# Moving the tiles that TensorE reads to other byte offsets in SBUF

## What is computed

```
h    = rmsnorm(x, a_norm);            xb, gate = h @ a_w_in           # 2048 -> 2 x 2560
xb   = causal width-4 depthwise conv(xb)
r, i = sigmoid(block_diag(xb, w_r)), sigmoid(block_diag(xb, w_i))     # 10 blocks of 256
y    = linear recurrence over time of (a(r), u(i, xb));  x += (y * silu(gate)) @ a_w_out
k, v = rmsnorm(x, kv_norm) @ w_kv;    q, gate = rmsnorm(x, b_norm) @ b_w_in
o    = stick-breaking attention(q, k, v)                              # 16 heads of 128
x   += (o * silu(gate)) @ b_w_out;    out = rmsnorm(x, final_norm)
```

## The kernel before

| tiles | offset modulo 512 |
|---|---|
| `stage`, `w_hi`, `w_lo`, `x_hi`, `x_lo`, `ident` | 128 |
| `y_hi`, `y_lo`, `o_hi`, `o_lo`, `q`, `k`, `v`, `last` (hi and lo) | 320 |
| `xc_hi`, `xc_lo`, `wgt`, `wt_hi`, `wt_lo` | 352 |

## Time and profile before

### The profile page before, as it was taken

The page is one execution under the profiler, slowest core; times in us unless marked ns, Lnnn a source line. Parts: engine busy times, 40 slices in busy tenths (PEclk is TensorE's granted clock), DMA queues, the critical chain, the costliest instruction groups (busy, mean ns, idle before and its releaser), DMA issues.

```text
span 1712.9 us, 25540 instructions
## 1 busy us (share of the span) xinstructions
PE 1698.3 (99%) x8607; PEld 1445.6 (84%) x8607; DVE 908.6 (53%) x1688; ACT 799.0 (47%) x1622; POOL 228.1 (13%) x219
## 2 busy tenths in 40 slices
PE   8999999999999999999999999999999999999998
PEld 6888888888887888888889898888989898898888
DVE  5667666666675333354646455454645455453323
ACT  7555566666554233244445444453544444432223
POOL 0121121112211010121001010111101011113100
PEclk9999999999999999999999999999999999999999
DMA  5333333333332222223232222222232222323223
GB/s 184 101 99 99 97 98 92 96 89 97 105 99 92 95 95 92 92 82 104 78 95 79 91 87 80 86 81 90 82 94 81 86 91 75 99 74 111 90 95 136
DMA packets 155910, 162.22 MB, mean 95 GB/s; under 512 B 9608, under 2 KB 147032, under 8 KB 155736
## 3 DMA queue, kind: packets, MB, share of 16 engines
q1 hardware_dynamic: 155864, 161.63, 30.4%
HBM read 157.39 MB, written 4.19 MB: 94 GB/s over the span
## 4 chain that ended last, share of the span: by engine, by line
PE 98%; ACT 1%; DVE 0%; DMA 0%; issue 0%; POOL 0%; SPq 0%; POOLq 0%; DVEq 0%; ACTq 0%
PE ps L355 96%; PE ps L476 1%; DMA xraw<-in_x 0%; PE ps L531 0%; PE ps L384 0%; POOL y_lo L1168 0%; DVE rbuf L976 0%; ACT w_hi L589 0%; PE ps L391 0%; ACT abuf L673 0%; DVE w_lo L834 0%; DVE tbuf L972 0%; ACT L673 0%; ACT rbuf L661 0%; ACT tbuf L670 0%
## 5 line engine op out<-in xcount | busy, mean ns | idle before, releaser
L355 PE MATMUL ps<-x_hi,w_hi 128*128 128x512 f32 x1408 | 550.9, 391 | 0.0
L355 PE MATMUL ps<-x_hi,w_lo 128*128 128x512 f32 x1408 | 548.1, 389 | 0.0
L355 PE MATMUL ps<-x_lo,w_hi 128*128 128x512 f32 x1408 | 548.1, 389 | 0.0
L837 DVE SCALAR_TENSOR_TENSOR w_lo<-stage,cT,w_hi 128x256 fp32r<-128x256 f32 x416 | 230.6, 554 | 504.1 <-ACT w_hi L593 503.5
L591 ACT ACTIVATE w_hi<-stage,cT 128x256 fp32r<-128x256 f32 x416 | 211.8, 509 | 486.1 <-PE ps L355 485.8
L355 PEld LDWEIGHTS ps<-x_hi,w_lo 128*128 128x128 f32 x1408 | 264.3, 188 | 55.3
L355 PEld LDWEIGHTS ps<-x_hi,w_hi 128*128 128x128 f32 x1408 | 264.4, 188 | 54.6 <-issue 0.7
L355 PEld LDWEIGHTS ps<-x_lo,w_hi 128*128 128x128 f32 x1408 | 264.4, 188 | 54.2 <-issue 0.5
L834 DVE TENSOR_TENSOR w_lo<-stage,w_hi 128x512 fp32r<-128x512 f32 x160 | 127.8, 800 | 251.8 <-ACT w_hi L589 251.8
L589 ACT ACTIVATE w_hi<-stage 128x512 fp32r<-128x512 f32 x160 | 100.8, 632 | 272.7 <-PE ps L355 271.1
L839 DVE SCALAR_TENSOR_TENSOR w_lo<-stage,cT,w_hi 128x256 fp32r<-128x256 f32 x416 | 213.4, 513 | 0.0
(11 more groups left out here) (161 smaller groups left out, 1995.8 us busy)
## 6 DMA issues: line engine op xcount, KB each, us to landing
stage<-in_a_w_in SPq DMA_DIRECT2D x160, 256.0 KB, 2.7
stage<-in_b_w_in SPq DMA_DIRECT2D x128, 256.0 KB, 2.6
stage<-in_w_kv SPq DMA_DIRECT2D x128, 256.0 KB, 2.6
stage<-in_a_w_out SPq DMA_DIRECT2D x80, 256.0 KB, 2.5
stage<-in_b_w_out SPq DMA_DIRECT2D x64, 256.0 KB, 3.0
out<-x SPq DMA_DIRECT2D x8, 512.0 KB, 3.3
xraw<-in_x SPq DMA_DIRECT2D x3, 1024.0 KB, 11.7
stage<-in_a_w_r SPq DMA_DIRECT2D x10, 256.0 KB, 3.0
```

What stands on the lines that cost most here:

```text
L355: mm = pe.matmul(dst, a, b, start=start and n == 0, stop=stop and n == 2, skip_group_check=not check)
L837: nc.vector.scalar_tensor_tensor(w_lo[:, slot, 0:256], stage[:, slot, 0:256], cT[:, col:col + 1], f(w_hi[:, slot, 0:256]), ALU.mult, ALU.s ...
```

## The change

Only the places of the tensors in SBUF change; no instruction is added, removed or moved. The small tensors go first, unused tensors (`gap`) are put between the tiles, some tiles of a scope change order, and `last_hi`, `last_lo` become the first four tiles of `x_hi`, `x_lo`. By the same rules of allocation the offsets modulo 512 become:

| tile | offset | tile | offset |
|---|---|---|---|
| `w_hi` | 0 | `w_lo` | 64 |
| `x_hi` (and `last_hi`) | 128 | `x_lo` (and `last_lo`) | 256 |
| `y_hi` | 256 | `y_lo` | 64 |
| `xc_hi` | 32 | `xc_lo` | 192 |
| `o_hi` | 128 | `o_lo` | 384 |
| `q`, `k`, `v`, `wt` (hi and lo), `wgt` | 384 | `ident` | 128 |
| `stage` | 0 | | |

```diff
--- before.py
+++ after.py
@@ -79,6 +79,7 @@
 WT_OFF = {0: 0, 1: 512, 3: 896, 2: 1024}
 BANK_COLS = ((4, 0, 512), (5, 512, 512), (6, 1024, 256))
 I_ORDER = (3, 2, 0, 1)
+LINE_GAP = 192
 LOG1P_TERMS = (1 / 17, 1 / 15, 1 / 13, 1 / 11, 1 / 9, 1 / 7, 1 / 5, 1 / 3)
 
 
@@ -88,16 +89,13 @@
         def sb(name, shape, dt=F32, scope=ctx):
             return scope.enter_context(nc.sbuf_tensor(name, shape, dt))
 
+        def gap(name, size, scope=ctx):
+            sb(name, [P, size // 4], F32, scope)
+
         def sem(name):
             return ctx.enter_context(nc.semaphore(name))
 
 
-        stage = sb("stage", [P, RING, 512])
-        w_hi = sb("w_hi", [P, RING, 512], F32R)
-        w_lo = sb("w_lo", [P, RING, 512], F32R)
-        x_hi = sb("x_hi", [P, KD, S], F32R)
-        x_lo = sb("x_lo", [P, KD, S], F32R)
-        rb = sb("rb", [P, S])
         ident = sb("ident", [P, P])
         ones = sb("ones", [P, P])
         cT = sb("cT", [P, NC])
@@ -109,10 +107,21 @@
         rs_tok = sb("rs_tok", [P, TT])
         small = sb("small", [P, 3, TT])
         ss5 = sb("ss5", [P, TT, 5])
+        gap("after_small", LINE_GAP)
+        rb = sb("rb", [P, S])
+        stage = sb("stage", [P, RING, 512])
+        w_hi = sb("w_hi", [P, RING, 512], F32R)
+        gap("before_w_lo", 64)
+        w_lo = sb("w_lo", [P, RING, 512], F32R)
+        gap("before_x_hi", 64)
+        x_hi = sb("x_hi", [P, KD, S], F32R)
+        gap("before_x_lo", 128)
+        x_lo = sb("x_lo", [P, KD, S], F32R)
 
 
         with ExitStack() as mem12:
             y_hi = sb("y_hi", [P, KR, S], F32R, mem12)
+            gap("before_y_lo", 320, mem12)
             y_lo = sb("y_lo", [P, KR, S], F32R, mem12)
             with ExitStack() as mem0:
                 xraw = sb("xraw", [P, TT, D], F32, mem0)
@@ -120,25 +129,27 @@
                 rows_b = sb("rows_b", [P, P], F32, mem0)
                 rows_g = sb("rows_g", [P, P], F32, mem0)
             with ExitStack() as mem1:
-                xbp = sb("xbp", [P, 2, S + 4], F32, mem1)
+                gap("before_xc_hi", 480, mem1)
+                xc_hi = sb("xc_hi", [P, 2, S], F32R, mem1)
+                gap("before_xc_lo", 160, mem1)
+                xc_lo = sb("xc_lo", [P, 2, S], F32R, mem1)
                 xc = sb("xc", [P, 2, S], F32, mem1)
-                xc_hi = sb("xc_hi", [P, 2, S], F32R, mem1)
-                xc_lo = sb("xc_lo", [P, 2, S], F32R, mem1)
                 gate = sb("gate", [P, 2, S], F32, mem1)
                 rbuf = sb("rbuf", [P, 2, S], F32, mem1)
                 tbuf = sb("tbuf", [P, 2, S], F32, mem1)
                 abuf = sb("abuf", [P, 2, S], F32, mem1)
+                xbp = sb("xbp", [P, 2, S + 4], F32, mem1)
             with ExitStack() as mem2:
                 x1 = sb("x1", [P, 2, S], F32, mem2)
                 sq = sb("sq", [P, 2, S], F32, mem2)
                 acc = sb("acc", [P, S], F32, mem2)
         with ExitStack() as mem34:
+            gap("before_o_hi", 384, mem34)
             o_hi = sb("o_hi", [P, HEADS, S], F32R, mem34)
+            gap("before_o_lo", 256, mem34)
             o_lo = sb("o_lo", [P, HEADS, S], F32R, mem34)
             x1_f = sb("x1_f", [P, 4, S], F32, mem34)
             with ExitStack() as mem3:
-                masked = sb("masked", [P, S], F32, mem3)
-                seen = sb("seen", [P, P], F32, mem3)
                 q_hi = sb("q_hi", [P, 2, S], F32R, mem3)
                 q_lo = sb("q_lo", [P, 2, S], F32R, mem3)
                 k_hi = sb("k_hi", [P, 2, S], F32R, mem3)
@@ -147,15 +158,16 @@
                 v_lo = sb("v_lo", [P, TT, 2 * P], F32R, mem3)
                 sg = sb("sg", [P, 2, S], F32, mem3)
                 kf = sb("kf", [P, 2, S], F32, mem3)
-                keep = sb("keep", [P, 1284], F32, mem3)
-                wgt = sb("wgt", [P, 1280], F32, mem3)
                 wt_hi = sb("wt_hi", [P, 1280], F32R, mem3)
                 wt_lo = sb("wt_lo", [P, 1280], F32R, mem3)
+                wgt = sb("wgt", [P, 1280], F32, mem3)
+                masked = sb("masked", [P, S], F32, mem3)
+                seen = sb("seen", [P, P], F32, mem3)
+                keep = sb("keep", [P, 1284], F32, mem3)
             with ExitStack() as mem4:
                 x2 = sb("x2", [P, TT, D], F32, mem4)
                 g_fin = sb("g_fin", [P, D], F32, mem4)
-                last_hi = sb("last_hi", [P, 4, 512], F32R, mem4)
-                last_lo = sb("last_lo", [P, 4, 512], F32R, mem4)
+        last_hi, last_lo = x_hi[:, 0:4, :], x_lo[:, 0:4, :]
         ib = xbp[:, :, 3:3 + S]
 
         ps = [ctx.enter_context(nc.psum_tensor(f"ps{b}", [P, S], F32)) for b in range(8)]
```

## The result

Slower: 1723.92 us (median of 4 runs, 1723.73 to 1725.16) against 1715.64 us before on the same chip (4 runs), a ratio of 1.005 with the 95% interval 1.0038 to 1.0062. The profiled execution's span goes from 1712.9 to 1722.1 us. The forecast was 1690.2 us, with 0.55 for faster.

The account below looks back on a forecast made before the run. It took one unbroken TensorE matmul stream, set by start-to-start distance, as the bound; less extra in x, y, xc, w against o and v summed to 25.3 us, from 1715.5 to 1690.2 us, range 1654 to 1742.

Parts of the forecast that it names:

- What bounds the kernel: Whole span: some 1,698 us are one stream of matmuls; time changes only with the distance between matmul starts.
- the other edits: `last_hi`, `last_lo` on x tiles, and other engines' new addresses: costed at nothing.
- the choice between the bounds: New pairs' extra, between none (114 us less) and 20.0 ns (44 us more): took 11.1 ns from a 256-column row.
- the x streams: 4224 matmuls of 512 columns streaming x: extra from 13.3 to 11.1 ns, 9.4 us less.
- y: Streams of y: 640 matmuls save 5.7 us, the 320 that still agree save 2.1 us.
- xc: Streams of xc: 240 matmuls at 8.9 ns less each, 2.1 us less.
- w against o at 512 columns: Phase 4, 576 matmuls streaming w against o: 4.4 ns less each, 2.6 us less.
- the v units: 1536 matmuls of 256 columns streaming w against x: 2.2 ns less each, 3.4 us less.
- 256 columns against o: w streamed against o with 256 columns: already at 11.1 ns extra, so nothing gained.
- The third, a difference costs: Rival: agreement at 128 is good, x goes the way of y; 24.8 us slower, 1740.3 us; chance 0.28.
- The second, the place of the streamed tile: Rival: only the streamed tile's place counts, whatever the weights; y_hi improves 4.3 us, 1711.2 us; chance 0.17.
- the first, own ports: Rival: each stream has its own port, offsets are not the cause; no change, 1715.5 us; chance 0.10.

Follow-up runs that it names:

- the grid: TensorE-only kernels, one streamed against one weight tile, 64 offset pairs modulo 512; 512 columns: 227.2 ns agreeing, 233.3 ns at 192; 256 columns: 120.0 agreeing.
- the finer steps: TensorE-only kernel, one weight tile at 0, streamed tiles at 0, 16 ... 240, five lengths; 192 and 128 columns: 111 to 112 ns anywhere.
- The table of three products: TensorE-only kernels, order hi.hi, hi.lo, lo.hi, hi weights at 0, other tiles at 64 offset cases; 512 columns: mean 231.7 ns, all agreeing 226.7.
- 64/128/0: Product case, lo weights/hi stream/lo stream modulo 256, hi weights at 0: x after the change; table 230.1 ns, kernel 229.2.
- 0/192/192: Product case, lo weights/hi stream/lo stream modulo 256, hi weights at 0: y before the change; table 233.5 ns, kernel 233.3.

## Why the prediction was wrong

**What bounds the kernel** held. The time is the sum of the distances between starts, 9.2 us more in them and 9.2 us more in the span, with TensorE's waits at 7.1 us and the clock unchanged. That the other edits cost nothing held as far as the account can tell.

**The step that failed** is the choice between the bounds: "Between them I take 11.1 ns, the smallest extra that a row shows", and "That is the one clean comparison at equal length". The comparison was clean, and true: at 256 columns tiles 64 apart have 117.8 ns and agreeing ones 120.0, as the grid found. But it was carried over to 512 columns, where the order is the other way round: 227.2 agreeing, 228.8 at 64, 232.4 and 233.3 beyond. 4224 matmuls of 512 columns hung on a row of 256 columns, while three of the four streams of that very length (228.9, 233.3, 233.3 for tiles that differ) pointed the other way from x (226.7, tiles agree); only the short scores did not. In place of 9.4 us less the x streams took 10.2 more, a difference of 19.6 of the 33.7 us by which forecast and result are apart. The extra at 256 columns may be made of something else: in the finer steps 128 and 192 columns take 111 to 112 ns as well, only 2 ns below the best place of 256, so at 256 the columns may not be what the extra comes on top of. That this turns the order round isn't shown.

**The other terms.** y: 7.8 us less forecast, 2.0 measured; xc: 2.1, measured 0.0; w against o at 512 columns: 2.6 less, measured 1.2 more; the v units: 3.4 less, measured 0.0; 256 columns against o: nothing, measured 0.1. All rested on the same 11.1 ns, but for 2.1 us of y, which gave `y_lo` the 13.3 ns of an agreeing pair.

**Which tiles act.** I took a matmul's stream and the next weights for the pair that counts. The table of three products shows no such pair. By that reading, with the period of 256, y after would have agreed in all three of its transitions, and have had 227 ns; it had 231.1. The prediction also took y (stream at 320, weights at 128) and w against o (stream at 128, weights at 320) for the same difference of 192. Modulo 256 one stream is 192 ahead of its weights and the other 64, and the grid has 233.3 ns for the one and 228.8 for the other.

**The rivals.** The third, a difference costs, was right in kind and stood at 0.28. It was too large (24.8 us), since it gave x the distance of y; 64/128/0 isn't 0/192/192. Against it I had put w against o, whose low 11.1 ns is again the 256-column row. The second, the place of the streamed tile, fitted all rows of before, because w was always at 128: only a grid that moves both could part them, and in it, at 512 columns, the absolute place did nothing. For the first, own ports, the scores had spoken, which agree and had 20.0 ns. They are three matmuls between others; in a block of 24 the same pair, 320 and 320, has 227.2 ns. And such a block doesn't begin there: its first five distances are 226, 236, 228, 233 and 231 ns, and only then do they stay at 226 and 227. The scores' three are 233, 231 and 236. Three starts were too few to stand for a steady distance.

**Two rules cited.** By the Trainium skill ("SBUF — State Buffer", section "Who interferes with whom") the two read ports of TensorE are independent, and PE never waits on anyone. By that, offsets would change nothing; in these runs byte offsets alone moved the distance from 226.7 to 235.6 ns. Whether it is these two ports that meet, the runs don't show. The Trainium skill ("TensorE: Matmul & The Clock Gate", section "Back-to-back issue gap") gives 2.5 ns over the columns at the full clock. With float32r that was not reached at 512 columns at any place; the lowest was 5.3 ns, with the stream standing still.

**Open.** What makes the extra: the runs show a period of 256 bytes (with the two blocks of the grid outside it), values that move with 16 bytes, and that the stream must walk. They don't show which reads meet, if any do, or in which unit. Whether a better place than full agreement exists for 512 columns in steps finer than 64 bytes for all four tiles wasn't tried; for a single pair the only equal one was 240.

## What to carry to other kernels

In a kernel that is one unbroken stream of float32r matmuls, place moved the time from 1707 to 1734 us, 1.6%: keep the streamed and the weight tiles of 512-column products at one offset modulo 256, here 8.6 us less for 64 bytes of filler and two tensors put last. What a row shows for one length must not be carried to another length; and when single cases disagree, a kernel of one's own that walks the grid costs 400 us of chip time and leaves little room for choosing. Leave out the first matmuls of each block, and read no steady distance from three starts. Odd places are no neutral choice: they draw from a table whose mean is 5 ns worse than agreement.

## What the runs showed of the hardware

- The distance between starts follows the offsets of the tiles from one another modulo 256 bytes: 227 to 236 ns for 512 columns, 113 to 122 ns for 256, no effect for 192 and 128 columns (111 to 112 ns, one pair of tiles). For a single pair, absolute places made no more than 1.1 ns in the 64 blocks of 512 columns; with 256 columns two of 64 blocks were 4.4 ns off.
- The sign of the effect depends on the length: full agreement is best at 512 columns (226.7 ns), and 6.7 ns worse than the best place at 256 (120.0 against 113.3 ns).
- At 2.4 columns for each ns, the values that return are the columns and a multiple of 16 more (226.7 and 233.3 ns: 544 and 560), or lie a third or two thirds between. A steady mean can hold unequal distances that take turns, as 224, 228 and 234 ns in the x streams after.
- After another pair of tiles, an agreeing pair at 512 columns takes five to ten distances of 224 to 236 ns before it stays at 226 to 227.
- Hi and lo tiles act together; single-pair distances don't predict the distance of a product of three.
- With a streamed operand of step 0, 512 columns take 218.6 to 218.7 ns at all 16 pairs of offsets, whether the weights walk or not.
